# A two-block transformer kernel: expert down weights cut by output-column halves instead of rows, and the last expert finished half by half

## The chip, the cores and the metric

The kernel runs on one core of one Trainium2 chip, as one program with five instruction streams: TensorE (PE), VectorE (DVE), ScalarE (ACT), GpSimd (POOL) and SyncE (SP, which issues most transfers). The metric is the device time of one execution in microseconds. Before the change it was 996.03 us, the median of three runs (995.69 to 996.56).

## What is computed

Two blocks work on x, 256 tokens of 1024 channels, all in float32. The change lies in the last part of the second block, a mixture of 32 experts:

```python
# hn2: normed tokens; top-1 group of 4, then top-2 experts of the 8 in it
def run_block(xb, e):
    return (jax.nn.silu(xb @ w_gate[e]) * (xb @ w_up[e])) @ w_down[e]
# w_gate, w_up: (32, 1024, 512);  w_down: (32, 512, 1024)
ffn = sum over the two chosen experts of  weight * run_block(token, e)
x = x + gate2 * ffn
out = rms_norm(x, g_final)        # mean of squares over all 1024 columns
```

`gate2` is one of six pieces of 1024 columns of `silu(c) @ w_ada + b_ada`.

## The kernel before

**Stages.** The first 554 us of the profiled execution hold the first block and the attention part of the second. The rest is the expert loop (`blocks(0, NE)`, 32 experts one after the other) and a short end. A second loop, `blocks(NE, NOV)`, runs only if an expert gets more than 64 tokens; in the profiled execution it does not run.

**One expert.** Each expert has six weight pieces of 1 MB, 128 partitions of 2048 floats: four for gate and up, two for down. They lie one behind the other in `w_experts_2`, which the host lays out. SP reads them in order into 22 buffers (`er`), each used again when PE has finished with it (semaphore `eused`); late in the loop one transfer brings up to five pieces, and the last six pieces come one by one, the very last in two parts (`first0` announces its first half). On PE:

- `gate_up(j, 0)` and `gate_up(j, 1)`: 16 matmuls of 512 columns into one PSUM bank, gate in partitions 0 to 63, up in 64 to 127.
- `middle(j)`: two transposes of the product H; ACT copies the result to `HT` (`HL` for the last expert).
- `down(j)`: 8 matmuls of 512 columns. The piece `hf` holds 256 of the 512 rows of the down weights with all 1024 output columns; output columns 0 to 511 go to partitions 0 to 63 of one bank, 512 to 1023 to partitions 64 to 127.
- DVE (`down`) scales that bank by the slot weight and by gate2, ACT copies it to `Y` as a rounded high part, and DVE writes the low part `Y` (semaphore `yl`).
- `combine(j)`: four matmuls of 512 columns spread the 64 slots over the 256 tokens and add them to four banks `moe0` to `moe3` (bank `2t+q`: token half t, column half q), which hold x already. `comb_t0` and `comb` count their ends.

Every float32 matmul stands in the trace as two records with a weight load each; the two of a pair (partitions 0 to 63, and 64 to 127) run beside one another.

**The order.** It is written out by hand in `pe_program`. In the loop, `down(j - 1)` comes behind `gate_up(j, 1)` and `combine(j - 2)` before it. The end of the loop is `gate_up(31, 0)`, `middle(30)`, `combine(29)`, `gate_up(31, 1)`, first half of `down(30)`, `middle(31)`, second half of `down(30)`, `down(31)`, `combine(30)`, `combine_last(31)`. PE executes in this order, so a waiting instruction holds all behind it.

**The last expert** has no high and low parts: DVE scales its bank into `YS` in two column halves (`ys_half`, `ys`), and `combine_last` multiplies in full float32, with the partitions 0 to 63 and 64 to 127 of `YS` beside one another.

**The end.** When token half 0 is complete (`comb_t0`), ACT squares `moe0` and `moe1` with a row sum, and DVE multiplies them by g_final into `fin`, each engine one bank at a time and never the same one; then the same for token half 1 (`comb`). `mean`, `root` and `inverse` make the factor 1/rms of each token half; DVE scales the left 512 columns of `fin` and ACT the right ones; three transfers write the output, two from SP and one from ACT.

Of the kernel before, what the change touches and what calls it, by code (L numbers as in the profile page):

```python
# [8 lines left out]
F32 = DT.float32  # L9
# [4 lines left out]
ALU = mybir.AluOpType  # L14
# [6 lines left out]
NE = 32  # L21
# [81 lines left out]
class Kit:  # L103
# [331 lines left out]
    def place_psum(self):  # L435
# [104 lines left out]
        def block_uses(base, n):  # L540
            p0 = base // 4
            for q in range(4):
                use(f"gat{p0}_{q}", ((2, 3, 1, 2)[q], f"xt{q % 2}", 4 * p0 + q // 2 * 2 + 2))
            for j in range(base, base + n + 1):
                p = j // 4 + 1
                gathers = j % 4 == 3 and 4 * p < base + n
                if j < base + n:
                    use(f"gu{j}", (j % 2, "GU", j + 1))
                if j == 2:
                    use("over", (2, "count", 1))  # L550
                if j < base + n and j % 2 == 0:
                    use(f"turn{j // 2}", (3, "wsl", 2 * j + 4))
                if j > base:
                    use(f"hid{j - 1}", (2, "hf", j))
                for q in range(4 if gathers else 0):
                    use(f"gat{p}_{q}", ((j + 1) % 2, f"xt{q % 2}", 4 * p + q // 2 * 2 + 2))
                if j > base:
                    done = ("yl", 2 * self.parted(j - 1) + 2) if j < base + n else ("ys", j)
                    use(f"down{j - 1}", (3 if j < base + n else j % 2, *done))
# [5 lines left out]
def pe_program(e, K):  # L565
# [276 lines left out]
    def turn_decay():  # L842
        b = K.at["decay"][0]
        free("decay")
        for k, (row, sem, value) in enumerate((("i", "F", 2), ("w0", "E", 1))):
            e.wait_ge(S[sem], value)
            for t in range(2):
                m = e.transpose(b[:, 8 * k + 4 * t:8 * k + 4 * t + 4], K.R[row][:, 128 * t:128 * t + 128],
                                K.cst[0:4, CST["ident"]:CST["ident"] + 4])
        m.then_inc(S["dec_mm"], 1)  # L850
# [86 lines left out]
    e.matmul(K.at["shift"][0][:, 0:36], C("ones"), K.wrq[:, :], start=True, stop=True).then_inc(S["shift_mm"], 1)  # L937
# [109 lines left out]
    b = K.at["rank"][0]  # L1047
# [5 lines left out]
    def blocks(base, n):  # L1053
# [55 lines left out]
        def down(j, halves=(0, 1)):  # L1109

            if 0 in halves:
                free(f"down{j}")
                e.wait_ge(S["hf"], j + 1)
            b, HT = K.at[f"down{j}"][0], K.hidden(j)
            for hf in halves:
                i = K.piece_of[j, "d", hf]
                for c in range(2):
                    if i == K.n_static - 1 and c == 0:
                        e.wait_ge(S["first0"], 32)
                    elif c == (i == K.n_static - 1):  # L1120
                        e.wait_ge(*K.loaded(i))
                    for q in range(2):
                        m = e.matmul(b[64 * q:64 * q + 64, :], HT[:, c, hf, :],  # L1123
                                     K.weights(i)[:, 1024 * c + 512 * q:1024 * c + 512 * q + 512],
                                     start=hf == 0 and c == 0, stop=hf == 1 and c == 1)
# [12 lines left out]

        def combine_last(j):

            e.wait_ge(S["pt"], 2 * j + 2)
            e.wait_ge(S["ys_half"], 1 if j < NE else 2)
            for t, c0, c1 in ((0, 0, 256), (0, 256, 512), (1, 0, 512)):
                if c0:
                    e.wait_ge(S["ys"], j + 1)
                pt = K.PT[j % 4][:, 128 - 128 * t:256 - 128 * t]
                for q in range(2):
                    r = slice(64 * q, 64 * q + 64)
                    m = e.matmul(K.at[f"moe{2 * t + q}"][0][:, c0:c1], pt[r, :].bitcast(F32), K.YS[r, c0:c1], start=False,
                                 stop=True, skip_group_check=True)  # L1150
                if c1 == 512:
                    m.then_inc(S["comb" if t else "comb_t0"], 1)
# [6 lines left out]
        for j in range(base + 1, base + n - 1):  # L1159
# [19 lines left out]
            down(j - 1)  # L1179
# [21 lines left out]
def act_program(e, K):  # L1201
# [413 lines left out]
    def blocks(base, n):  # L1615
        def turned_p(p):
            b = K.at[f"turn{p}"][0]
            e.wait_ge(S["turnP"], p + 1)
            if p > 1:
                e.wait_ge(S["comb"], 2 * p - 2)  # L1620
            for i in range(2):
# [69 lines left out]
    with e.If(count > 0):  # L1691
        blocks(NE, NOV)
        e.wait_ge(S["comb"], NE + NOV)
# [4 lines left out]
    for t in range(2):  # L1698
        e.wait_ge(S["comb" if t else "comb_t0"], NE)
        for n in range(2):  # L1700
            if n:
                e.wait_ge(S["fin"], 2 * t + 1)
            e.activation(K.sqx[:, t, 512 * n:512 * n + 512], K.at[f"moe{2 * t + n}"][0][:, :], ACT.Square,
                         scale=1.0 / 32, accum_out=stat(8 * t + n)).then_inc(S["sq"], 1)
            if t and n == 0:
                root(11, 0, 1)
# [8 lines left out]
def dve_program(e, K):  # L1715
# [400 lines left out]
    e.wait_ge(S["dec_mm"], 1)  # L2116
# [114 lines left out]
    e.wait_ge(S["shift_mm"], 1)  # L2231
# [184 lines left out]
    def blocks(base, n, rank):  # L2416
# [31 lines left out]
        def down(j):  # L2448
            e.wait_ge(S["eused"], K.piece_of[j, "d", 1] + 1)
# [4 lines left out]
            for o, sem in ((slice(0, 256), "ys_half"), (slice(256, 512), "ys")) if whole else ((slice(0, 512), "ys"),):  # L2454
                e.scalar_tensor_tensor(out=(K.YS if whole else b)[:, o], in0=b[:, o], scalar=K.wsl[:, j % 4:j % 4 + 1],  # L2455
                                       in1=K.gate2q[:, o], op0=ALU.mult, op1=ALU.mult).then_inc(S[sem], 1)
# [50 lines left out]
    with e.If(count > 0):  # L2507
# [22 lines left out]
        blocks(NE, NOV, ok)[1]()  # L2530
        e.wait_ge(S["comb"], NE + NOV)
    finish()


    e.wait_ge(S["comb_t0"], NE)
    e.wait_ge(S["l_cst"], 32)

    def gained(t, n):
        if n == 0:
            e.wait_ge(S["sq"], 30 + 2 * t)  # L2540
# [3 lines left out]
    def mean(t):  # L2544
        k = 8 * t
        e.wait_ge(S["sq"], 31 + 2 * t)
# [8 lines left out]
    def scaled(t):  # L2555
        k = 8 * t
        e.wait_ge(S["rs"], 11 + t)
        e.wait_ge(S["fin"], 2 * t + 2)
# [197 lines left out]
def lay_out(inputs):  # L2756
# [13 lines left out]
    down = i["w_expert_down_2"][0].reshape(NE, 2, 2, 128, 1024).transpose(3, 0, 1, 2, 4)  # L2770
# [3 lines left out]
    arrays["w_experts_2"] = experts  # L2774
    arrays["norm_final_g"] = arrays["norm_final_g"].reshape(1, -1)
# [23 lines left out]
```

## Time and profile before

| quantity | value |
|---|---|
| median of 3 runs | 996.03 us (995.69 to 996.56) |
| the profiled execution's own time | 997.51 us |
| its span, first to last instruction | 995.6 us |
| mean granted TensorE clock | 0.994 |
| PE busy | 972.7 us, 98% |
| DVE / ACT busy | 57% / 42% |
| read from HBM | 326.39 MB |

The span is 1.9 us shorter than the time of the same execution; the rest lies before the first and behind the last instruction. Busy time is the union of records, and since matmuls are pipelined a busy PE need not be PE at its peak; what sets the time of a stretch is seen from the waits and from the chain. DMA and GB/s are given for 40 equal slices of 24.9 us.

### The profile page before, as it was taken

The numbers are of one execution on the slowest core, as the hardware profiler recorded it, in microseconds if no ns is written. First come the engines' busy times: TensorE is split into PE (matmuls) and PEld (weight loads), VectorE is DVE, ScalarE is ACT, GpSimd is POOL, SyncE is SP. The second block draws the span as 40 slices with busy tenths as digits, with TensorE's granted clock in tenths as the row PEclk, the third lists the DMA queues.
The fourth block names the chain that finished last, engine by engine and source line by source line (L and its number), as shares of the span: only waits on it lengthen the run. The fifth ranks groups of instructions, "written<-read, shape, count | busy, mean of one in ns | idle before, by whom it ended". The sixth has DMA issues, their size and how long they took to land.

```text
span 995.6 us, 12470 instructions
## 1 busy us (share of the span) xinstructions
PE 972.7 (98%) x4936; PEld 637.1 (64%) x4936; DVE 565.6 (57%) x883; ACT 414.6 (42%) x650; POOL 84.7 (9%) x72
## 2 busy tenths in 40 slices
PE   8999999999999999999999999999999999899986
PEld 6888888888888888889988544343434343334432
DVE  5668767898898877876986432323333222223222
ACT  6743654435644444576784423222322222122223
POOL 0122002303222202110000000000000000000000
PEclk9999999999999999999999999999999999999998
DMA  9987659995778887556558999999999999999995
GB/s 325 391 287 256 201 174 319 332 313 193 245 256 291 293 297 252 187 192 211 177 196 339 386 424 424 429 431 433 432 430 431 434 429 430 431 425 425 429 423 222
DMA packets 73599, 328.33 MB, mean 330 GB/s; under 512 B 4812, under 2 KB 4976, under 8 KB 61120
## 3 DMA queue, kind: packets, MB, share of 16 engines
q1 hardware_dynamic: 71504, 323.68, 83.1%
q0 software_dynamic: 1888, 3.54, 1.3%
q8 instruction: 41, 0.67, 0.3%
q10 hardware_dynamic: 144, 0.26, 0.1%
q14 instruction: 22, 0.18, 0.0%
HBM read 326.39 MB, written 1.07 MB: 329 GB/s over the span
## 4 chain that ended last, share of the span: by engine, by line
PE 85%; DMA 9%; DVE 3%; issue 1%; ACT 1%; SPq 0%; DVEq 0%; ACTq 0%
PE bank L1096 19%; PE bank L1123 9%; DMA er<-in_w_experts 8%; PE bank L603 7%; PE bank L606 7%; PE bank L600 7%; PE bank L786 6%; PE bank L684 5%; PE bank L1065 3%; PE bank L791 3%; PE bank L688 3%; PE bank L654 2%; PE bank L657 2%; PE bank L660 2%; PE bank L1135 2%
## 5 line engine op out<-in xcount | busy, mean ns | idle before, releaser
L1096 PE MATMUL bank<-er,XT 128*64 128x512 f32 x1024 | 235.4, 598 | 6.4 <-DMA er<-in_w_experts 6.1
L1744 DVE TENSOR_TENSOR wlo<-raw,whi 128x2048 fp32r<-128x2048 f32 x87 | 203.0, 2344 | 63.8 <-ACT whi L1209 63.6
L1209 ACT ACTIVATE whi<-raw 128x2048 fp32r<-128x2048 f32 x87 | 165.0, 1911 | 79.4 <-PE bank L606 33.7
L1096 PEld LDWEIGHTS bank<-er,XT 128*64 128x64 f32 x1024 | 70.0, 137 | 140.1 <-issue 131.2
L1123 PE MATMUL bank<-er,HT 128*64 128x512 f32 x496 | 112.3, 594 | 1.2 <-DMA er<-in_w_experts 1.2
L600 PE MATMUL bank<-whi,hh 128*128 128x512 f32 x224 | 88.4, 395 | 1.6 <-ACT whi L1216 1.6
L603 PE MATMUL bank<-wlo,hh 128*128 128x512 f32 x224 | 87.9, 393 | 0.2 <-DVE wlo L1753 0.2
L606 PE MATMUL bank<-whi,hl 128*128 128x512 f32 x224 | 88.0, 393 | 0.0
L1646 ACT ACTIVATE Y<-bank 64x512 fp32r<-64x512 f32 x62 | 36.7, 592 | 114.0 <-DVE bank L2455 113.2
L684 PE MATMUL bank<-f,whi 128*128 128x512 f32 x224 | 79.4, 398 | 0.0
L1123 PEld LDWEIGHTS bank<-er,HT 128*64 128x64 f32 x496 | 35.0, 137 | 68.6 <-issue 67.7
L1731 DVE SCALAR_TENSOR_TENSOR ada_acc<-raw,silu_c,ada_acc 128x512 f32<-128x512 f32 x96 | 75.7, 789 | 2.5
L2455 DVE SCALAR_TENSOR_TENSOR bank<-bank,wsl,gate2q 128x512 f32<-128x512 f32 x31 | 23.5, 759 | 91.3 <-PE bank L1123 91.3
L2438 DVE TENSOR_TENSOR H<-H,bank 128x256 f32<-128x256 f32 x32 | 13.5, 421 | 101.6 <-ACT H L1631 101.6
L688 PE MATMUL bank<-f,wlo 128*128 128x256 f32 x224 | 62.9, 281 | 0.0
L1631 ACT ACTIVATE H<-bank 128x256 f32<-128x256 f32 x32 | 12.3, 385 | 104.9 <-PE bank L1096 104.9
L2460 DVE TENSOR_TENSOR Y<-bank,Y 64x512 fp32r<-64x512 f32 x62 | 42.7, 689 | 21.4 <-ACT Y L1646 20.4
L786 PE MATMUL bank<-whi,zh 128*128 128x512 f32 x128 | 50.2, 392 | 0.0
L791 PE MATMUL bank<-wlo,zh 128*128 128x512 f32 x128 | 49.9, 390 | 0.0
L600 PEld LDWEIGHTS bank<-whi,hh 128*128 128x128 f32 x224 | 42.5, 190 | 10.3 <-ACT whi L1216 1.8
L684 PEld LDWEIGHTS bank<-f,whi 128*128 128x128 f32 x224 | 42.1, 188 | 10.4
L603 PEld LDWEIGHTS bank<-wlo,hh 128*128 128x128 f32 x224 | 42.4, 189 | 9.3 <-DVE wlo L1753 0.5
(387 smaller groups left out, 1581.7 us busy)
## 6 DMA issues: line engine op xcount, KB each, us to landing
er<-in_w_experts SPq DMA_DIRECT2D x27, 2048.0 KB, 37.9
er<-in_w_experts SPq DMA_DIRECT2D x49, 1024.0 KB, 9.4
er<-in_w_experts SPq DMA_DIRECT2D x12, 4096.0 KB, 33.6
raw<-in_w_in SPq DMA_DIRECT2D x41, 1024.0 KB, 6.3
er<-in_w_experts SPq DMA_DIRECT2D x8, 5120.0 KB, 28.5
raw<-in_w_ff SPq DMA_DIRECT2D x32, 1024.0 KB, 6.1
raw<-in_w_ada SPq DMA_DIRECT2D x24, 1024.0 KB, 6.2
raw<-in_w_out SPq DMA_DIRECT2D x8, 1024.0 KB, 6.8
```

What stands on the lines that cost most here:

```text
L600: e.matmul(o, a_h, r_h, start=start and c == 0, stop=False)
L603: e.matmul(o, a_h, r_l, start=False, stop=False)
L606: m = e.matmul(o, a_l, r_h, start=False, stop=stop and c == 3)
L684: e.matmul(b[q][:, :], w_h, x2[:, k, :, :].rearrange("p i n -> p (i n)"), start=k == 0, stop=False, skip_group_check=True)
L688: m = e.matmul(b[q][:, 0:256], w_l, x2[:, k, 0, :], start=False, stop=k == 7, skip_group_check=True)
L786: m = e.matmul(o, a, whi[s][:, r], start=p == 0 and f == 0 and which == 0, stop=p == 7 and f == 3 and which == 1)
L791: m = e.matmul(o, a, wlo[s][:, r], start=False, stop=False)
L1096: m = e.matmul(b[64 * w:64 * w + 64, :], K.XT[:, j % 5, k, :], K.weights(i)[:, o:o + 512], start=k == 0, stop=k == 7)
L1123: m = e.matmul(b[64 * q:64 * q + 64, :], HT[:, c, hf, :], K.weights(i)[:, 1024 * c + 512 * q:1024 * c + 512 * q + 512], start=hf == 0 and ...
L1209: e.activation(whi[K.ring(n)][:, :], raw[h.raw][:, :], ACT.Copy).then_inc(S["hi"], 1)
L1731: e.scalar_tensor_tensor(out=acc[:, :], in0=raw[h.raw][:, 512 * c:512 * c + 512], scalar=K.sc[:, 4 * k + c:4 * k + c + 1], in1=acc[:, :], ...
L1744: e.tensor_tensor(wlo[K.ring(n)][:, :], raw[h.raw][:, :], whi[K.ring(n)][:, :].bitcast(F32), ALU.subtract).then_inc(S["lo"], 1)
```

## The change

The two down pieces of an expert now hold 512 output columns each with all 512 rows, not 256 rows with all columns (`down(j, h, parts)`: piece h, four row groups g of 128). Inside a piece, columns 0 to 255 go to partitions 0 to 63 (q = 0) and 256 to 511 to partitions 64 to 127. So every matmul of `down` has 256 columns, and there are 16 of them for an expert, not 8. `combine` has eight matmuls of 256 columns, not four of 512, since a 256-column piece of Y now belongs to bank `2t + h`, columns `256q`. The host swaps the middle 256-column quarters of gate2 in `w_ada_2` and `b_ada_2` to match. Number and size of the transfers stay.

The last expert has a PSUM bank for each column half. Its two halves are computed, scaled, combined and squared one after the other. `combine_last(j, h)` has four matmuls; the third waits until the first two have ended (`comb_two`). The end works by column half: ACT squares and DVE multiplies the two token halves of columns 0 to 511 first, then of 512 to 1023; both means come at the end. Two single-use semaphores are merged into `small_mm`, which changes no order.

```diff
-        def down(j, halves=(0, 1)):
...
-            for hf in halves:
-                i = K.piece_of[j, "d", hf]
-                for c in range(2):
...
-                    for q in range(2):
-                        m = e.matmul(b[64 * q:64 * q + 64, :], HT[:, c, hf, :],
-                                     K.weights(i)[:, 1024 * c + 512 * q:1024 * c + 512 * q + 512],
+        def down(j, h, parts=range(4)):
+            use, whole = K.at[f"down{j}"], j == base + n - 1
...
+            b, HT, i = use[h if whole else 0], K.hidden(j), K.piece_of[j, "d", h]
+            for g in parts:
+                if i == K.n_static - 1 and g < 2:
+                    e.wait_ge(S["first0"], 32)
+                else:
+                    e.wait_ge(*K.loaded(i))
+                for q in range(2):
+                    m = e.matmul(b[64 * q:64 * q + 64, 256 * h:256 * h + 256], HT[:, g % 2, g // 2, :],
+                                 K.weights(i)[:, 512 * g + 256 * q:512 * g + 256 * q + 256],
...
         def combine(j):
...
-                    m = e.matmul(K.at[f"moe{2 * t + q}"][0][:, :], K.PT[j % 4][:, 128 - 128 * t:256 - 128 * t], K.Y[q][:, :],
-                                 start=False, stop=False, skip_group_check=True)
+                    for h in range(2):
+                        m = e.matmul(K.at[f"moe{2 * t + h}"][0][:, 256 * q:256 * q + 256],
+                                     K.PT[j % 4][:, 128 - 128 * t:256 - 128 * t], K.Y[q][:, 256 * h:256 * h + 256],
...
+        def combine_last(j, h):
+            if h:
+                e.wait_ge(S["ys"], j + 1)
+            else:
+                e.wait_ge(S["pt"], 2 * j + 2)
+                e.wait_ge(S["ys_half"], 1 if j < NE else 2)
+            for n, (t, q) in enumerate(((0, 0), (1, 1), (0, 1), (1, 0))):
+                if n == 2:
+                    e.wait_ge(S["comb_two"], 6 * (j // NE) + 3 * h + 2)
+                r = slice(64 * q, 64 * q + 64)
+                m = e.matmul(K.at[f"moe{2 * t + h}"][0][:, 256 * q:256 * q + 256],
+                             K.PT[j % 4][r, 128 - 128 * t:256 - 128 * t].bitcast(F32), K.YS[r, 256 * h:256 * h + 256],
+                             start=False, stop=True, skip_group_check=True)
+                m.then_inc(S["comb_two" if n < 3 else "comb" if h else "comb_t0"], 1)
...
-        down(j - 1, (0,))
+        down(j - 1, 0)
         middle(j)
-        down(j - 1, (1,))
-        down(j, (0, 1))
+        down(j - 1, 1)
+        down(j, 0)
         combine(j - 1)
-        combine_last(j)
+        down(j, 1, (0, 1))
+        combine_last(j, 0)
+        down(j, 1, (2, 3))
+        combine_last(j, 1)
...
# ACT, the end
-    for t in range(2):
-        e.wait_ge(S["comb" if t else "comb_t0"], NE)
-        for n in range(2):
-            if n:
-                e.wait_ge(S["fin"], 2 * t + 1)
+    for n in range(2):
+        e.wait_ge(S["comb_two"], 3 * n + 3)
+        e.wait_ge(S["comb" if n else "comb_t0"], NE)
+        for t in range(2):
+            if t:
+                e.wait_ge(S["fin"], 2 * n + 1)
...
# DVE, the end
-    gained(0, 1)
+    gained(1, 0)
     gained(0, 0)
-    mean(0)
+    e.wait_ge(S["comb_two"], 6)
     e.wait_ge(S["comb"], NE)
     gained(1, 1)
-    gained(1, 0)
+    gained(0, 1)
+    mean(0)
+    mean(1)
     inverse(0)
-    mean(1)
     scaled(0)
```

On PE, at the end of the loop from `down(31)` on, stood before (L1123 is `down`, L1135 `combine`, L1149 `combine_last`; HL is the last expert's hidden tile, Y and YS the scaled results, PT the slot-to-token matrix; x3 means three more of the kind):

```order
L1123 MATMUL bank<-er_187,HL 64x512 [waits e_10,hf,GU]
L1123 MATMUL bank<-er_187,HL 64x512 x3
L1123 MATMUL bank<-er_187,HL 64x512 [waits first0]
L1123 MATMUL bank<-er_187,HL 64x512
L1123 MATMUL bank<-er_187,HL 64x512 [waits e_whi0]
L1123 MATMUL bank<-er_187,HL 64x512
L1135 MATMUL bank<-Y_175,PT_181 128x512 [waits yl,pt]
L1149 MATMUL bank<-YS,PT_182 128x256 [waits ys_half,pt]
L1149 MATMUL bank<-YS,PT_182 128x256
L1149 MATMUL bank<-YS,PT_182 128x256 [waits ys]
L1149 MATMUL bank<-YS,PT_182 128x256
L1149 MATMUL bank<-YS,PT_182 128x512 x2
```

At the same place, from the first matmul of `combine(30)` on, now stands (L1140 is `combine`, L1126 `down`, L1156 `combine_last`; before these rows lie the eight matmuls of `down(31, 0)`, and seven more L1140 follow its first row):

```order
L1140 MATMUL bank<-Y_175,PT_181 128x256 [waits yl,pt]
L1126 MATMUL bank<-er_187,HL 64x256 [waits first0,hf,GU]
L1126 MATMUL bank<-er_187,HL 64x256 [waits first0]
L1156 MATMUL bank<-YS,PT_182 128x256 [waits ys_half,pt]
L1156 MATMUL bank<-YS,PT_182 128x256 [waits comb_two]
L1126 MATMUL bank<-er_187,HL 64x256 [waits e_whi0,hf]
L1126 MATMUL bank<-er_187,HL 64x256 [waits e_whi0]
L1156 MATMUL bank<-YS,PT_182 128x256 [waits ys]
L1156 MATMUL bank<-YS,PT_182 128x256 [waits comb_two]
```

`combine(30)` has moved from behind all of `down(31)` to behind its first half, and the second half of `down(31)` now stands behind that wait for `yl`, cut in two by the first half of `combine_last`.

On DVE, at the end, stood before (L2455 scales the last expert's halves, L2541 multiplies by g_final, L2547 is `mean`, L2553 `inverse`, L2559 `scaled`):

```order
L2455 SCALAR_TENSOR_TENSOR YS<-bank,wsl,gate2q 128x256 [waits yl,wsl,eused]
L2455 SCALAR_TENSOR_TENSOR YS<-bank,wsl,gate2q 128x256
L2541 TENSOR_TENSOR fin<-bank,gfb 128x512 [waits l_cst,comb_t0]
L2541 TENSOR_TENSOR fin<-bank,gfb 128x512 [waits sq]
L2547 SCALAR_TENSOR_TENSOR st<-st 128x1 [waits sq]
L2541 TENSOR_TENSOR fin<-bank,gfb 128x512 [waits comb]
L2541 TENSOR_TENSOR fin<-bank,gfb 128x512 [waits sq]
```

and now stands (L2476 scales, L2564 multiplies, L2570 is `mean`):

```order
L2476 SCALAR_TENSOR_TENSOR YS<-bank,wsl,gate2q 128x256 [waits eused,yl,wsl]
L2476 SCALAR_TENSOR_TENSOR YS<-bank,wsl,gate2q 128x256 [waits eused]
L2564 TENSOR_TENSOR fin<-bank,gfb 128x512 [waits l_cst,comb_t0,comb_two]
L2564 TENSOR_TENSOR fin<-bank,gfb 128x512 [waits sq]
L2564 TENSOR_TENSOR fin<-bank,gfb 128x512 [waits comb,comb_two]
L2564 TENSOR_TENSOR fin<-bank,gfb 128x512 [waits sq]
L2570 SCALAR_TENSOR_TENSOR st<-st 128x1 [waits sq] x2
```

The second scaling has a wait of its own, for the second column half of `down(31)`, and all multiplications by g_final stand behind it.

## Rows read from the trace of the kernel before

**Rows 1.** The page: slices of 24.9 us, DMA share in tenths and rate.
```profile
DMA  9987659995778887556558999999999999999995
GB/s 325 391 287 256 201 174 319 332 313 193 245 256 291 293 297 252 187 192 211 177 196 339 386 424 424 429 431 433 432 430 431 434 429 430 431 425 425 429 423 222
```

**Rows 2.** PE's waits, 556 to 985 us: total us, times, longest.
```profile
PE bank L1096 <- DMA er<-in_w_experts: 6.1, 4, 3.7
PE bank L1123 <- DMA er<-in_w_experts: 1.2, 1, 1.2
```

**Rows 3.** Stretches: from:to, length, busy us by engine, granted clock, DMA share, GB/s.
```profile
855.30:859.60 4.30, 0.59 (x6) 0.02 (x2) 1.38 (x2) 0.88 (x2) 0.00 (x0) 1.00 1.01 434
859.60:864.00 4.40, 4.40 (x16) 2.12 (x17) 0.00 (x0) 0.00 (x0) 0.00 (x0) 0.61 1.00 432
963.07:967.97 4.90, 3.65 (x16) 1.26 (x17) 0.76 (x1) 0.42 (x1) 0.00 (x0) 1.00 0.99 415
967.97:982.40 14.43, 14.43 (x66) 5.32 (x68) 3.02 (x5) 2.99 (x7) 0.00 (x0) 1.00 0.93 384
```

**Rows 4.** The chain that ended last: start us, us, what.
```profile
516.64 2.75 PE bank L924 x32
563.10 3.58 PE bank L1096 x16
587.29 3.43 PE bank L1123 x16
865.73 1.21 PE bank L1065 x8
985.17 1.09 PE bank L1149 x8
```

**Rows 5.** Groups by form, L924 and L1149: count, busy us, mean ns.
```profile
L924 PE MATMUL bank<-PTt,vat 128*64 128x256 f32 x16 | 2.5, 385 | 0.0
L924 PE MATMUL bank<-PTt,vat 128*64 128x128 f32 x16 | 1.6, 272 | 0.0
L1149 PE MATMUL bank<-YS,PT 64*128 64x256 f32 x8 | 1.1, 402 | 0.0
```

**Rows 6.** Timeline of PE, a gather and a combine: start us, us, what.
```profile
561.89 0.39 PE L1065 MATMUL bank<-PP,th 128*128 128x256 f32 x1
...
563.03 3.65 PE L1096 MATMUL bank<-er,XT 128*64 128x512 f32 x16
...
971.76 1.17 PE L1135 MATMUL bank<-Y,PT 128*128 128x512 f32 x4
...
972.86 3.65 PE L1096 MATMUL bank<-er,XT 128*64 128x512 f32 x16
```

**Rows 7.** Timeline of all engines, 980 us to the end.
```profile
980.39 3.65 PE L1123 MATMUL bank<-er,HL 128*64 128x512 f32 x16
981.93 1.41 DVE L2460 TENSOR_TENSOR Y<-bank,Y 64x512 fp32r<-64x512 f32 x2 [0.66 <-ACT Y L1646]
982.76 0.40 PEld L1123 LDWEIGHTS bank<-er,HL 128*64 128x64 f32 x4 [0.46 <-DMA er<-in_w_experts]
983.97 1.20 PE L1135 MATMUL bank<-Y,PT 128*128 128x512 f32 x4
984.08 0.88 DVE L2455 SCALAR_TENSOR_TENSOR YS<-bank,wsl,gate2q 128x256 f32<-128x256 f32 x2 [0.74 <-PE bank L1123]
985.10 1.99 PE L1149 MATMUL bank<-YS,PT 64*128 64x256 f32 x12
986.28 1.42 DVE L2541 TENSOR_TENSOR fin<-bank,gfb 128x512 f32<-128x512 f32 x2 [1.32 <-PE bank L1149]
989.54 1.32 ACT L1710 ACTIVATE fin<-fin,st 128x512 f32<-128x512 f32 x2
989.92 0.49 DVE L2559 TENSOR_SCALAR fin<-fin,st 128x512 f32<-128x512 f32 x1
990.49 1.80 SPq L2723 DMA_DIRECT2D out<-fin  x1
```

More of the change, by code:

```diff
@@ L557, in block_uses @@
                 if j > base:
-                    done = ("yl", 2 * self.parted(j - 1) + 2) if j < base + n else ("ys", j)
-                    use(f"down{j - 1}", (3 if j < base + n else j % 2, *done))
+                    if j < base + n:
+                        use(f"down{j - 1}", (3, "yl", 2 * self.parted(j - 1) + 2))
+                    else:
+                        use(f"down{j - 1}", (0, "ys_half", 1 if base == 0 else 2), (1, "ys", j))
         block_uses(0, NE)
@@ L936, in pe_program @@
     e.wait_ge(S["router"], ROUTER["sum"])
-    e.matmul(K.at["shift"][0][:, 0:36], C("ones"), K.wrq[:, :], start=True, stop=True).then_inc(S["shift_mm"], 1)
+    e.matmul(K.at["shift"][0][:, 0:36], C("ones"), K.wrq[:, :], start=True, stop=True).then_inc(S["small_mm"], 1)
     def turn_h(t):
@@ L1134, in combine @@
                 for q in range(2):
-                    m = e.matmul(K.at[f"moe{2 * t + q}"][0][:, :], K.PT[j % 4][:, 128 - 128 * t:256 - 128 * t], K.Y[q][:, :],
-                                 start=False, stop=False, skip_group_check=True)
+                    for h in range(2):
+                        m = e.matmul(K.at[f"moe{2 * t + h}"][0][:, 256 * q:256 * q + 256],
+                                     K.PT[j % 4][:, 128 - 128 * t:256 - 128 * t], K.Y[q][:, 256 * h:256 * h + 256],
+                                     start=False, stop=False, skip_group_check=True)
                 m.then_inc(S["comb" if t else "comb_t0"], 1)
[L1139 to L1152, printed above, removed]
+        def combine_last(j, h):
+            if h:
+                e.wait_ge(S["ys"], j + 1)
+            else:
+                e.wait_ge(S["pt"], 2 * j + 2)
[8 more added lines that the diff above has]
+                m.then_inc(S["comb_two" if n < 3 else "comb" if h else "comb_t0"], 1)
         gather(base // 4, 0)
@@ L1184, in blocks @@
         gate_up(j, 1)
-        down(j - 1, (0,))
+        down(j - 1, 0)
         middle(j)
-        down(j - 1, (1,))
-        down(j, (0, 1))
+        down(j - 1, 1)
+        down(j, 0)
         combine(j - 1)
-        combine_last(j)
+        down(j, 1, (0, 1))
+        combine_last(j, 0)
+        down(j, 1, (2, 3))
+        combine_last(j, 1)
     e.wait_ge(S["tl"], 2)
@@ L2453, in down @@
             b, whole = K.at[f"down{j}"][0], j == base + n - 1
-            for o, sem in ((slice(0, 256), "ys_half"), (slice(256, 512), "ys")) if whole else ((slice(0, 512), "ys"),):
-                e.scalar_tensor_tensor(out=(K.YS if whole else b)[:, o], in0=b[:, o], scalar=K.wsl[:, j % 4:j % 4 + 1],
-                                       in1=K.gate2q[:, o], op0=ALU.mult, op1=ALU.mult).then_inc(S[sem], 1)
+            if not whole:
+                e.wait_ge(S["eused"], K.piece_of[j, "d", 1] + 1)
+                e.scalar_tensor_tensor(out=b[:, :], in0=b[:, :], scalar=K.wsl[:, j % 4:j % 4 + 1], in1=K.gate2q[:, :],
+                                       op0=ALU.mult, op1=ALU.mult).then_inc(S["ys"], 1)
+            if whole and base:
+                e.wait_ge(S["comb_two"], 6)
+            for h in range(2 if whole else 0):
+                o = slice(256 * h, 256 * h + 256)
+                e.wait_ge(S["eused"], K.piece_of[j, "d", h] + 1)
+                e.scalar_tensor_tensor(out=K.YS[:, o], in0=K.at[f"down{j}"][h][:, o], scalar=K.wsl[:, j % 4:j % 4 + 1],
+                                       in1=K.gate2q[:, o], op0=ALU.mult, op1=ALU.mult).then_inc(S["ys" if h else "ys_half"], 1)
             for q in range(0 if whole else 2):
@@ L2530, in dve_program @@
         blocks(NE, NOV, ok)[1]()
+        e.wait_ge(S["comb_two"], 12)
         e.wait_ge(S["comb"], NE + NOV)
     finish()
+    e.wait_ge(S["comb_two"], 3)
     e.wait_ge(S["comb_t0"], NE)
@@ L2774, in lay_out @@
     arrays["w_experts_2"] = experts
+    for name in ("w_ada_2", "b_ada_2"):
+        gate = arrays[name][..., 5120:6144]
+        gate = gate.reshape(*gate.shape[:-1], 2, 2, 256).swapaxes(-3, -2).reshape(gate.shape)
+        arrays[name] = np.ascontiguousarray(np.concatenate([arrays[name][..., 0:5120], gate], axis=-1))
     arrays["norm_final_g"] = arrays["norm_final_g"].reshape(1, -1)
```

38 lines of the change are left out of this document (18 added, 20 removed).

## The prediction

> **What bounds the kernel now.** I read the slices of the page first, then PE's waits, the stretches, the chain, and last the timeline of the end. The slices show two regimes: before slice 22 the transfer rate varies, from slice 24 (about 600 us) on it stays at 424 to 434 GB/s with a DMA share of nine tenths or more [rows 1]. From there to the end of the expert weights the transfers are at their rate. PE is almost as full: from 556 to 985 us it waits for weights five times, 7.3 us in all (6.1 + 1.2) [rows 2]. So the expert loop is held by the transfers, with PE 7.3 us short of holding it itself. The reader is to see that the last such wait ends at 967.97 us (1.25 us of the 4.90 us from 963.07 are free of PE work) and that PE then works without a break: 14.43 us busy in 14.43 us [rows 3]. What is behind 967.97 us is PE's, and at its very end a chain over PE, DVE and ACT. The last weights arrive when the load at 982.76 us is released, and its matmuls start 0.2 us later, so in the last expert transfers and PE are level [rows 7].
>
> **The change in the loop.** The matmuls of down get twice as many and half as wide. Before, the 16 records of an expert (512 columns each) take 3.43 us, and 0.15 us more when matmuls of another shape stand before them (3.58) [rows 4]; that is 8192 record columns, 0.42 ns each. No row shows 32 records of 256 columns with 64 weight columns, but L924 has this shape: 16 records of 256 and 16 of 128 columns, 6144 record columns, in 2.75 us [rows 4, 5]. At 0.42 ns they cost 2.57 us; with the entry of 0.15 us that leaves 0.03 us over 32 records. Lower bound of the extra: nothing. Upper bound: L924's whole rate, 2.75 / 6144 x 8192 = 3.67 us, so +0.24 us. I take +0.03, because L924 contains one entry, which down has already.
>
> Combine goes from four matmuls of 512 columns to eight of 256. The gather L1065 has just this shape and number. Start to next line's start it takes 563.03 - 561.89 = 1.14 us, the combine before takes 972.86 - 971.76 = 1.10 us [rows 6]: +0.04 us. The bound below is zero, since the columns are the same; the bound above is twice the matmuls at the old cost each, +1.1 us, which the gather rules out; with a wait before it the gather takes 1.21 us [rows 4], so +0.11 at most.
>
> Together +0.07 us an expert, 29 experts before 967.97 us: 2.0 us of PE work, 10 us at the upper ends (0.24 + 0.11). The 7.3 us in which PE waits for weights hide the 2.0 us. The cover is gone from 0.25 us an expert on; at the upper ends 2.9 us would come through. There is also work to get back: after the wait of 3.7 us the granted clock is 0.61 for 4.4 us, which is near the lower level, 1.2 GHz, and PE had been idle before it fell [rows 3]; a shorter wait there may keep it at 2.4 GHz. Number, size and order of transfers stay. So up to 967.97 us: zero.
>
> The Trainium skill (TensorE: Matmul & The Clock Gate, section "The mechanism") says that a weight load overlaps running matmuls only when its row group differs. All of down's matmuls use all rows. By that rule none of its loads would be hidden, and twice the loads would cost twice the load time. The trace disagrees: 16 records with a load each take exactly the time of their columns, and L924 at half the width nearly so [rows 4, 5]. What the rule would give is the fourth case below.
>
> **The change in the end.** I go through PE's order, before and after.
> 1. down(31) starts at 980.39 us [rows 7]; after it is +0.07 (combine(29) and down(30)): 980.46.
> 2. Its first half takes 1.72 us: PE is through at 982.2.
> 3. Next in PE's queue is combine(30), which waits for `yl`. DVE finishes it at 981.93 + 1.41 = 983.34 us [rows 7], after down(30), ACT's copy and two subtractions, which the change leaves as they are; +0.06 makes 983.40. Before, the 3.65 us of down(31) covered this. Now PE stands 1.2 us, and the second half of down(31), which needs nothing from DVE, stands behind it. PE goes on at 983.45 (a handover is 0.04 to 0.05 us, as from PE's end 984.04 to DVE's start 984.08 [rows 7]).
> 4. combine(30), eight matmuls behind a wait: 1.21 us [rows 4]: 984.66.
> 5. Two of four row groups of the second half: entry 0.15 + 0.86 = 1.01: 985.67.
> 6. combine_last(31, 0). `ys_half` is ready (DVE 983.4 + 0.44). Eight records of this kind take 1.09 us, 0.54 for four, and one lasts 0.40 [rows 4, 5]. The third matmul waits for the ends of the first two: 0.27 + 0.40 + 0.05 = 0.72, then 0.54: 986.93.
> 7. The other two row groups: 0.15 + 0.86, and 0.22 until the last result stands (3.65 against 3.43): 988.16. The data came at 982.8, it does not matter here.
> 8. DVE scales half 1: 0.44 us, with two handovers 0.53: 988.69.
> 9. combine_last(31, 1): 0.72 + 0.27 + 0.40 = 1.39: 990.1 us. Before, the last combine ended at 985.10 + 1.99 = 987.09 [rows 7]. That is **+3.0 us**, of it 1.2 from the wait in 3, 0.9 from the two waits of PE for itself (0.45 each), the rest from DVE's scaling, which now lies alone between two pieces of PE work, and from entries.
>
> Then the column order should pay. ACT squares token half 0 of columns 0 to 511 at 987.2, but the square of token half 1 waits for DVE's first product, and DVE's queue has the scaling of step 8 before it: product 988.7 to 989.4 (0.71 [rows 7]), second square to 990.1. So the first half is just off the path at 990.1. Behind the last combine: square, square, 0.70 each, with handovers to 991.6; means, root and reciprocal to 992.25 (0.65); scaling of the left columns 0.49, reciprocal, scaling 0.49: 993.35. Before, the last scaling ended at 989.92 + 0.49 = 990.41, 3.32 us behind the last combine; now 3.25. The last SP transfer, which waits for it, moves from 990.49 to 993.4. ACT's right half moves from 990.86 (989.54 + 1.32) to 993.55. Gain of the new order 0.1 to 0.2 us.
>
> **Sum:** 0 + 3.0 - 0.15 = **+2.85 us**, take 2.8. The profiled execution goes from 997.51 to 1000.3 (span 998.4); it stands 1.48 us above the median, so the median goes from 996.03 to **998.8 us**. Bounds of the end: if PE's self-waits cost nothing and entries neither, +1.5; if a half combine takes 0.3 more each time, +3.5.
>
> **Rivals.**
> *No change.* The wait for `yl` or the self-waits are cheaper than I read. Without the 1.2 and the 0.9 the sum is +0.7 us, 996.7. Against it: DVE's 983.34 is a measured end and PE cannot pass it.
> *The half order wins (not slower).* Its place is the last landing L. From L to the last combine the old order needs 987.09 - 982.76 = 4.3 us; the new one, if PE stands ready at step 7's matmuls, needs 1.2 + 0.53 + 1.4 = 3.1 and then 0.1 less: 1.3 us gained, 994.7 us. PE reaches these matmuls at 986.9, so this holds in full only if weights land after 987, and it breaks even at L = 990.1 - 4.3 - 0.1 = 985.7, 3 us later than the trace has it. For it: transfers are the bound of the whole loop. Against it: their rate and bytes stay, and the trace has them in at 982.8.
> *PE becomes the bound of the loop.* If narrow matmuls cost the upper ends, 2.9 us come through on top: 1001.7. If loads do not hide (the page's rule, worked out as a mechanism of this kernel: eight more pairs of loads an expert, each as long as the load group at 982.76 for four, 0.40, thus 0.2 a pair), 1.6 us an expert, 51 us, less 7.3: 1043 us. L924 speaks against both.
>
> **How the numbers follow.** About 2 us, 0.2%, is what a measurement of this kernel can tell from no change. Forecast 78% (with its own spread of 0.8 us, a sixth of it below +2 us); no change 10%; half order wins 6%; PE the bound 6%, of it one for unhidden loads. Slower by over 0.2%: 0.65 + 0.06 = 0.71. Faster: 0.04, from the third case with a late landing and from errors in all steps. Same: 0.25. The range reaches from the no-change case less some scatter, 996.3, to just under the upper ends, 1001.4.
>
> **What would show it.** In the changed profile: down's 32 records an expert in 3.4 to 3.5 us; waits for weights in the loop 4 to 6 us in all, not 7.3; the last group of them still ending near 968 us; a PE wait at `combine` (L1140) for DVE `Y` of about 1.2 us near 983; last combine near 990.1; span near 998.4. I am wrong if PE starts gate_up(31, 0) later than 968.5, if there is no PE idle time between 982 and 983.4, if the last combine ends before 989, or if the rate of the last slices differs.

## The result, and the profile after

The changed kernel takes 1000.66 us in the median of six runs (999.2 to 1003.5), the kernel before 996.15 us (six runs): ratio 1.0046, 95% interval 1.0035 to 1.0056. It is slower by 4.5 us. Two more series, r1 and r3 below, gave 1.0038 (1.0022 to 1.0055) and 1.0030 (1.0020 to 1.0041), 3 to 4 us. A ratio of 1.0010 is 1 us. The ratios are not the quotients of the medians; for a kernel with few runs the two can differ by 0.0017, and where they tell different things both are given. Times and ratios here are of runs in the fast state; one run of before (1167 us) and one of loop_only (2176 us) in series r3 were slow. The forecast was 998.8 us, +2.8; the time of 1000.66 us lies inside the range, near its upper end.

The profiled execution took 999.30 us, with a span of 997.5 us. The page, slices of 24.9 us as in [rows 1]:

```profile
DMA  9987559985688886655658999999999999999994
GB/s 330 391 305 257 184 169 352 327 297 207 211 287 300 298 277 231 221 195 172 211 204 324 394 424 423 427 439 428 426 434 426 439 424 431 433 423 426 426 423 172
```

From slice 23 on the transfers run at 423 to 439 GB/s, as before. PE's waits from 556 to 988 us, against [rows 2] (L1098 is gate_up, L1140 combine, L1126 down):

```profile
PE bank L1098 <- DMA er<-in_w_experts: 5.8, 3, 3.3
PE bank L1140 <- DVE Y L2481: 1.3, 1, 1.3
PE bank L1126 <- DMA er<-in_w_experts: 1.0, 1, 1.0
```

There are still 6.8 us of waits for weights (before: 7.3), and one new wait, for Y. The groups by form, against [rows 4, 5]:

```profile
L1126 PE MATMUL bank<-er,HT 128*64 128x256 f32 x992 | 112.9, 380 | 1.0 <-DMA er<-in_w_experts 1.0
L1140 PE MATMUL bank<-Y,PT 128*128 128x256 f32 x248 | 37.0, 291 | 1.3 <-DVE Y L2481 1.3
```

The same view of the kernel before has 112.3 and 36.4 us for these two groups, at half the count (496 and 124). Twice the matmuls at half the width cost 0.6 us and 0.6 us over the whole loop, so 0.02 us each an expert.

The end of the loop and the end, against [rows 7] (timeline: start us, us, engine, line, operation; L1156 is combine_last, L2476 the scaling of a column half, L2564 the product with g_final):

```profile
967.42 3.65 PE L1098 MATMUL bank<-er,XT 128*64 128x512 f32 x16 [1.24 <-DMA er<-in_w_experts]
...
979.80 1.95 PE L1126 MATMUL bank<-er,HL 128*64 128x256 f32 x16
...
981.50 1.41 DVE L2481 TENSOR_TENSOR Y<-bank,Y 64x512 fp32r<-64x512 f32 x2 [0.66 <-ACT Y L1659]
...
983.06 1.19 PE L1140 MATMUL bank<-Y,PT 128*128 128x256 f32 x8 [1.31 <-DVE Y L2481]
...
984.18 1.08 PE L1126 MATMUL bank<-er,HL 128*64 128x256 f32 x8
...
985.19 1.50 PE L1156 MATMUL bank<-YS,PT 64*128 64x256 f32 x8
...
986.62 1.08 PE L1126 MATMUL bank<-er,HL 128*64 128x256 f32 x8
...
987.75 0.48 DVE L2476 SCALAR_TENSOR_TENSOR YS<-bank,wsl,gate2q 128x256 f32<-128x256 f32 x1 [4.26 <-PE bank L1126]
988.15 1.28 DVE L2564 TENSOR_TENSOR fin<-bank,gfb 128x512 f32<-128x512 f32 x2
988.29 1.50 PE L1156 MATMUL bank<-YS,PT 64*128 64x256 f32 x8 [0.59 <-DVE YS L2476]
...
993.03 0.46 SPq L2747 DMA_DIRECT2D out<-fin  x1
```

The reader is to see three things. The last wait for weights ends at 967.42 us, not later than before (967.97). PE stands 1.31 us before combine(30), while the second half of down(31) is behind it in the queue. And PE then hands to DVE and takes back (987.70 to 988.29). From 967.42 to the issue of the last SP transfer, 993.03, are 25.61 us; before it is 990.49 - 967.97 = 22.52 us [rows 3, 7]. So this chain is **3.1 us** longer. In this pair of executions the spans differ by 1.9 us only: the changed kernel's chain began 0.55 us sooner, and what comes behind the last issue was 0.65 us shorter. The kernel before has a single trace, and it is 1.4 us above its median of 996.15 us; so the chains can be compared with it, but what differs before and behind the chain can't be read from this pair.

PE's wait for itself is in the waits of 979 to 990 us:

```profile
PEld bank L1140 <- issue: 1.7, 1, 1.7
PE bank L1140 <- DVE Y L2481: 1.3, 1, 1.3
PEld bank L1156 <- DVE YS L2476: 1.0, 1, 1.0
PEld bank L1156 <- PE bank L1156: 1.0, 2, 0.5
```

The last row is the third matmul of each combine_last, held until the first two have ended: twice 0.5 us in which no weights are loaded.

### The profile page after: what moved, and what is told of

It is laid out like the page before. It is cut to its first block and busy times, and to the rows that moved or that the text cites. A ratio compares the mean times of both kernels' runs of the same rounds, so it can differ in the third digit from the quotient of the medians.

```text
span 997.5 us, 13786 instructions
## 1 busy us (share of the span) xinstructions
PE 974.4 (98%) x5576; PEld 684.0 (69%) x5576; DVE 565.8 (57%) x883; ACT 415.1 (42%) x650; POOL 84.8 (9%) x72
## 5 line engine op out<-in xcount | busy, mean ns | idle before, releaser
L1098 PE MATMUL bank<-er,XT 128*64 128x512 f32 x1024 | 236.1, 600 | 6.1 <-DMA er<-in_w_experts 5.8
L1098 PEld LDWEIGHTS bank<-er,XT 128*64 128x64 f32 x1024 | 70.3, 137 | 122.3 <-issue 107.3
L1126 PE MATMUL bank<-er,HT 128*64 128x256 f32 x992 | 112.9, 380 | 1.0 <-DMA er<-in_w_experts 1.0
L1126 PEld LDWEIGHTS bank<-er,HT 128*64 128x64 f32 x992 | 70.9, 137 | 46.9 <-issue 15.1
```

The lines of the kernel that those rows point to most:

```text
L1098: m = e.matmul(b[64 * w:64 * w + 64, :], K.XT[:, j % 5, k, :], K.weights(i)[:, o:o + 512], start=k == 0, stop=k == 7)
L1126: m = e.matmul(b[64 * q:64 * q + 64, 256 * h:256 * h + 256], HT[:, g % 2, g // 2, :], K.weights(i)[:, 512 * g + 256 * q:512 * g + 256 * q ...
```

## The experiments

Theory A: PE's order at the end makes the change slower, the loop costs nothing since it waits for weights. Theory B: the narrow matmuls in the loop cost time. As a third case from the prediction: the new order pays if the weights come late.

The labels r1, r2 and r3 name three series; all kernels of a series ran on one chip beside the kernel before, each series on another chip. The table holds the traced pieces: from gate_up(31, 0), where the last wait for weights ends, to down(31) (I), to the end of combine_last (II), to the issue of the last SP transfer (III), their sum, and from there to the end of the span (IV). Where a kernel was traced more than once, the values of I to III agreed within 0.04 us.

| kernel | I | II | III | sum | IV | ratio to before (95%) |
|---|---|---|---|---|---|---|
| before | 12.42 | 6.70 | 3.40 | 22.5 | 5.1 | |
| loop_only | 12.42 | 6.74 | 3.40 | 22.6 | 4.6, 4.9 | 1.0006 (0.9996 to 1.0015), 1.0018 (1.0006 to 1.0030) |
| old_order | 12.40 | 7.49 | 3.30 | 23.2 | 5.7, 5.2 | 1.0026 (1.0014 to 1.0037), 1.0024 (1.0015 to 1.0033) |
| interleaved | 12.37 | 6.75 | 4.11 | 23.2 | 5.8 | 1.0015 (1.0003 to 1.0028) |
| covered | 12.40 | 8.17 | 3.24 | 23.8 | 5.9 | 1.0019 (1.0002 to 1.0035) |
| comb_late | 12.37 | 8.99 | 3.24 | 24.6 | 5.6, 4.3 | 1.0049 (1.0033 to 1.0066), 1.0042 (1.0029 to 1.0055) |
| changed | 12.39 | 9.98 | 3.24 | 25.6 | 4.5, 4.4, 5.4 | 1.0046, 1.0038, 1.0030 (as above) |

**The changed kernel again**, unedited, twice.

> The changed kernel, unedited, for more executions and a second trace. The first trace explains +2.5 us of the end (last expert's first matmul 979.80 to span 997.5: 17.7 us; before 980.39 to 995.6: 15.2), while the median of six is +4.5 us. Theory A (the end alone, plus now and then a stretch of lower granted clock): this trace again has 17.5 to 18 us from that matmul to the end, and what is above lies in a stretch of clock 0.5 to 0.6 that the other trace lacks, or in a later last wait for weights. Theory B (the loop is slower): the last expert starts over 1 us later than 980.4 with the clock at 1.0 throughout. Median 999.5 to 1001.5.

> The changed kernel once more, to pool its time with the two series before. Theory A (its trace: +3.1 us from the last wait for weights to the issue of the last output transfer, 25.61 against 22.52 us): ratio to before 1.003 to 1.004, and those 25.6 us again. Theory B (a further cost that the traces do not show): 1.0045 or more again.

Medians 1000.25 and 999.03 us. The chain is 25.61 and 25.63 us, so what the trace shows of the end is the same each time; neither shows a stretch of low clock that would explain more. Theory A stands for the chain. The +3.0 us of r3 is the chain's +3.1; of the +3.8 us of r1 and the +4.5 us of the result, 0.7 and 1.4 us are not covered by it.

**loop_only**: the kernel before with narrow matmuls and nothing else.

```diff
-                    for q in range(2):
-                        m = e.matmul(b[64 * q:64 * q + 64, :], HT[:, c, hf, :],
-                                     K.weights(i)[:, 1024 * c + 512 * q:1024 * c + 512 * q + 512],
+                    for s_ in range(2):
+                        for q in range(2):
+                            o = 1024 * c + 512 * q + 256 * s_
+                            m = e.matmul(b[64 * q:64 * q + 64, 256 * s_:256 * s_ + 256], HT[:, c, hf, :],
+                                         K.weights(i)[:, o:o + 256],
...
# combine: likewise, two matmuls of 256 columns for each of 512
```

> The kernel before with only the narrow matmuls of the change: down 16 matmuls of 256 columns, combine eight of 256, same row pieces, same order, same end. Theory A: the loop's extra PE work (0.035 us an expert in the first trace) lies under the waits for weights, so within 0.4 us of before: 996.2 to 996.6. Theory B (narrow matmuls cost time that the one trace did not show, by longer loop or lower clock): +1.5 to +2.5 us, 997.7 to 998.7.

> Narrow matmuls alone, once more. Theory A: ratio 1.0000 to 1.0005, 22.6 us from the last wait for weights to the last output issue. Theory B (narrow matmuls carry the part of the cost that is missing in the traces): 1.001 or more.

The chain is 22.6 us, like before. The times are 996.75 us (before 996.7) in r1 and 997.12 us (before 995.75) in r3: +0.6 us by the ratio (-0.4 to 1.5) in the one series, +1.8 us (0.6 to 3.0) in the other. One of the eleven runs of r3, 1001.51 us, had a granted clock of 0.947, where the others have 0.994 to 0.998; it raises the second ratio. By the bounds set ahead of it, r3 came out as Theory B said (1.001 or more) and r1 as Theory A did. So the traces say that the narrow matmuls cost the chain nothing, and the times leave room for about 1 us outside it. A cost of that size is neither shown nor excluded.

**old_order**: the changed kernel with PE's old order; column pieces, combining and squaring by column half stay.

```diff
         down(j, 0)
+        down(j, 1)
         combine(j - 1)
-        down(j, 1, (0, 1))
         combine_last(j, 0)
-        down(j, 1, (2, 3))
         combine_last(j, 1)
```

> The changed kernel with PE's old order at the end: down(31) whole, combine(30), then both halves of combine_last; column pieces, narrow matmuls, combining and squaring by column half stay. Theory A (+3.0 us of the end come from PE's wait for Y, and DVE's second scaling alone between pieces of PE work): no wait for Y, DVE scales both halves under combine(30); last combine at 987.7 to 988.0, 2.0 us less than the changed kernel, +0.7 to +1.0 us against before. Rival (narrow matmuls and column order cost it, not PE's order): stays within 0.7 us of the changed kernel.

> Column pieces with PE's old order, once more. Theory A (its trace: 23.2 us from the last wait to the last output issue, +0.7 over before): +0.5 to +1.2 us over before in time. Rival (its first series, +2.6 us, holds; the column pieces cost 1 to 2 us outside the traced chain): +2 us or more again.

```profile
982.84 1.01 DVE L2475 SCALAR_TENSOR_TENSOR YS<-bank,wsl,gate2q 128x256 f32<-128x256 f32 x2
983.26 1.22 PE L1140 MATMUL bank<-Y,PT 128*128 128x256 f32 x8
984.41 2.73 PE L1156 MATMUL bank<-YS,PT 64*128 64x256 f32 x16
986.04 2.71 DVE L2563 TENSOR_TENSOR fin<-bank,gfb 128x512 f32<-128x512 f32 x4 [2.19 <-PE bank L1156]
...
990.44 0.39 SPq L2746 DMA_DIRECT2D out<-fin  x1
```

In the chain Theory A is right: the wait for Y is gone, DVE scales both halves under combine(30), and of the 3.1 us 2.4 are back. In time it is 2.0 us (1000.25 to 998.29) and 0.75 us (999.03 to 998.28) faster than the changed kernel by the medians, 1.2 and 0.6 us by the ratios. Against before it is 2.6 and 2.4 us slower by the ratios, where the chain says 0.7. So the rival of r3, that the column pieces cost 1 to 2 us outside the traced chain, came out as it was written; what that cost is stays open.

**comb_late**: combine(30) behind two more row groups.

```diff
         down(j, 0)
-        combine(j - 1)
         down(j, 1, (0, 1))
+        combine(j - 1)
         combine_last(j, 0)
```

> The changed kernel with combine(30) moved behind the first two row groups of the second half of down(31). Theory A (PE's 1.3 us wait for Y holds these matmuls back): they fill the wait, 0.9 to 1.0 us less than the changed kernel. Rival (what sets the end is not PE but DVE's and ACT's queue behind the scaling): under 0.3 us less.

> combine(30) behind the first two row groups of the second half, once more, since its first series scattered over 4.5 us. Theory A (its trace: 1.0 us less than the changed kernel up to the last output issue, 24.6 us): 0.7 to 1.3 us faster than r3_after. Rival: no faster than r3_after again, then the gap is given back in the output transfers.

The wait falls from 1.31 to 0.47 us, and combine_last ends 0.99 us sooner, as expected:

```profile
979.99 2.81 PE L1126 MATMUL bank<-er,HL 128*64 128x256 f32 x24
...
983.27 1.18 PE L1140 MATMUL bank<-Y,PT 128*128 128x256 f32 x8 [0.47 <-DVE Y L2481]
```

The time does not follow: 999.84 and 1000.04 us, against 1000.25 and 999.03 us of the changed kernel, so no faster. I had expected 0.7 to 1.3 us. For the first trace a part of it is seen behind the last issue, below; for the second it is not, and no run explains it.

**interleaved**: old order, and the pairs of the two halves of combine_last in turn, so that PE never waits for itself.

```diff
+        down(j, 1)
         combine(j - 1)
...
+        combine_last(j, 0, (0,))
+        combine_last(j, 1, (0,))
+        combine_last(j, 0, (1,), 2)      # comb_two >= 2
+        combine_last(j, 1, (1,), 4)      # comb_two >= 4
...
# combine_last takes the pairs it issues; ACT and DVE wait for 5 and 6 of comb_two, not 3 and 6
```

> Old order on PE (down(31) whole, combine(30)), and the two halves of combine_last interleaved, pair 1 of half 0, pair 1 of half 1, pair 2 of half 0, pair 2 of half 1, so that PE never waits for its own matmuls. Theory A: against r1_old_order (7.49 us from down(31)'s first matmul to the end of combine_last) two self-waits of 0.4 us go: 6.7 to 6.9 us, like the kernel before (6.70); 0.7 us faster than r1_old_order, within 0.5 us of before. Rival (the column pieces and the end by column half cost more than PE's order): the trace is as said, but the time stays at r1_old_order's +1.5 to +2.5 us over before.

combine_last ends 6.75 us behind down(31)'s first matmul, 0.74 us sooner than in old_order; that is what two self-waits are worth on PE. Nothing of it arrives: piece III grows from 3.30 to 4.11 us. The ends of PE's and DVE's work show why:

```profile
983.92 2.00 PE L1158 MATMUL bank<-YS,PT 64*128 64x256 f32 x16
985.62 2.71 DVE L2567 TENSOR_TENSOR fin<-bank,gfb 128x512 f32<-128x512 f32 x4 [2.26 <-PE bank L1158]
...
990.03 0.39 SPq L2750 DMA_DIRECT2D out<-fin  x1
```

The four products take 2.71 us without a gap from 985.62 us on. The first column half is ready only 0.3 us before the second. From down(31)'s first matmul (979.17 us) to the first product it is 6.45 us, in old_order 6.39 us (979.65 to 986.04), so the first half comes no sooner; and from there to the last SP issue it is 4.41 us here and 4.40 us there. So in both kernels the path runs from the first half on over DVE and ACT, not over PE, and in old_order the self-wait in the second half was hidden already. In time it is 1.6 us slower than before (997.84 against 996.24 us), which is the rival's case: the trace as said, the time not back.

**covered**: the new order without its self-wait in the first half, the second pair of combine_last(31, 0) behind the last row groups of down, and combine(30) as in comb_late.

```diff
         down(j, 0)
-        combine(j - 1)
         down(j, 1, (0, 1))
-        combine_last(j, 0)
+        combine(j - 1)
+        combine_last(j, 0, (0,))
         down(j, 1, (2, 3))
+        combine_last(j, 0, (1,))
         combine_last(j, 1)
...
# combine_last takes the pairs it issues
```

> The changed kernel's idea without two of its waits: down(31) first half and two row groups, combine(30), first pair of combine_last(31, 0), last two row groups, second pair of combine_last(31, 0), combine_last(31, 1). Theory A: from down(31)'s first matmul to the end of combine_last 8.99 us (r1_comb_late) less one self-wait, 8.5 to 8.7; the remaining +1.9 over before are the wait for Y (0.5), DVE's lone scaling (1.0 with the self-wait that follows) and shape entries. Rival: PE's self-wait had been hidden, then 9.0.

8.17 us, 0.3 to 0.5 less than expected: besides the self-wait, the pair now runs while DVE scales the second half. In the chain this is the best of the new order's three versions, 0.6 us behind old_order and 1.3 us behind before. By time it can't be told from old_order: 1.0019 (1.0002 to 1.0035) against 1.0026 and 1.0024. Its expectation had said 8.5 to 8.7 us, its rival 9.0; it was neither.

**Late weights.** SP issues 2 MB of other transfers (1.5 MB to unused places, and g_final) before the second half of the last weight transfer, once in the kernel before and once in the changed one.

```diff
             e.dma_start(K.weights(i)[:, 0:1024], src[:, 0:1024]).then_inc(S["first0"], 16)
+            e.wait_ge(S["gat"], NE)
+            e.dma_start(K.pad0[:, :], A["w_experts_2"][:, 1, 0, :]).then_inc(S["s_out"], 16)
+            e.dma_start(K.pad1[:, :], A["w_experts_2"][:, 2, 0, 0:1024]).then_inc(S["s_out"], 16)
+            e.dma_start(K.gfb[:, :], A["g_final_2"].broadcast_to([128, 1024])).then_inc(S["l_cst"], 16)
             e.dma_start(K.weights(i)[:, 1024:2048], src[:, 1024:2048]).then_inc(sem, 16)
...
# the transfer of g_final behind the loop goes; two unused places are declared
```

> The kernel before with the second half of its last weight transfer made late: SP issues 1.5 MB of transfers to unused places and the 0.5 MB of g_final ahead of it, 2 MB at 0.43 MB/us, so that it lands 4.9 us later, near 988. Theory A: the old end needs 4.3 us from the last landing to the end of combine_last, which ends near 992: +4.5 to +5 us over before.

> The changed kernel with the same late last transfer. Theory A: PE's waits of the new order now lie before the landing; from it to the end of combine_last 3.1 us, near 991, +1 to +1.5 us over the changed kernel and 0.8 to 1.5 us faster than r2_before_late: the new order pays only for late weights. Rival (the new order is worse wherever the weights land): slower than r2_before_late by 0.5 us or more.

Medians 1003.22 us (ratio 1.0054, 1.0033 to 1.0074) and 1000.4 us (1.0039, 1.0027 to 1.0052): now the changed order is the faster one, by 2.8 us in the medians and 1.5 us in the ratios, whose intervals overlap. The timelines, first of before with late weights, then of the changed kernel with late weights:

```profile
980.49 2.80 PE L1125 MATMUL bank<-er,HL 128*64 128x512 f32 x12
...
987.82 1.98 PE L1125 MATMUL bank<-er,HL 128*64 128x512 f32 x4 [4.53 <-DMA er<-in_w_experts]
989.72 2.08 PE L1137 MATMUL bank<-Y,PT 128*128 128x512 f32 x4
...
997.64 0.39 SPq L2727 DMA_DIRECT2D out<-fin  x1
```

```profile
986.09 1.08 PE L1128 MATMUL bank<-er,HL 128*64 128x256 f32 x8 [0.60 <-DMA er<-in_w_experts]
...
992.49 0.40 SPq L2751 DMA_DIRECT2D out<-fin  x1
```

The old order stands 4.53 us in one piece before its last matmuls. The new one has work until the landing and waits 0.60 us. From the end of the last wait at gate_up(31, 0) to the last SP issue it is 29.6 us (968.07 to 997.64) against 26.3 us (966.22 to 992.49): the new order wins 3.3 us. I had worked out 1.3 for the full case; the rest is the clock, which fell to its lower level in the old order's long wait. From its landing to the end of combine_last the old order takes 6.42 us (987.82 to 994.24), where the kernel before takes 4.3, so 2.1 of the 3.3 us are the clock. Stretches of before with late weights, columns as in [rows 3]:

```profile
983.30:987.80 4.50, 0.00 (x0) 0.00 (x0) 0.13 (x1) 0.81 (x2) 0.00 (x0) 0.80 0.36 147
987.80:991.20 3.40, 3.38 (x8) 1.46 (x8) 0.88 (x2) 0.00 (x0) 0.00 (x0) 0.50 0.00 0
```

At 0.50, 1.2 GHz, the combine takes 2.08 us and not 1.20. The landing itself, counted from the end of the last wait at gate_up(31, 0), is at 19.75 us in the one and 19.87 us in the other, so the comparison is a fair one.

## Why the prediction came out as it did

**The loop: right.** 0.07 us an expert was forecast, all hidden. Measured are 0.04 (two groups, 0.02 each), hidden: the last wait for weights ends at 966.2 to 967.8 us in all traces of the changed end. The granted clock after the long wait fell in the first trace and not in the two others (below), without any effect on the last wait: from the loop's first gate_up matmul to the end of that wait it is 412.5, 412.4 and 412.5 us. The fourth case, loads that are not hidden, is refuted by the 112.9 us. The waits for weights are 6.8 us in the first trace and 8.8 and 8.9 us in the two others, all outside my 4 to 6. The loop began at 554.6 to 555.3 us in these traces and at 557.0 us in the one of before, so PE came to the weights earlier and waited longer, and in the first trace the low clock filled a part of the waits; I had taken the start for given.

**The wait for Y: right.** 1.2 us forecast, 1.31 measured. DVE finishes at 981.50 + 1.41 = 982.91 us, PE goes on at 983.06, and moving combine(30) behind 0.86 us of matmuls (comb_late) takes 0.84 of the wait away. The case of no change, which needed this wait or the self-waits to be cheap, is refuted by the two.

**The self-waits and DVE's lone scaling: right in kind, a little small.** I had the end of PE's combine_last 9.6 us behind down(31)'s start; it is 9.98. The missing 0.4 us are three pieces. combine(30) starts 3.26 us behind down(31), not 2.99: Y is finished 0.17 us later, and PE starts 0.15 us behind DVE's end, where I had put 0.05 from a handover in the other direction. DVE's turn takes 0.59 us instead of 0.53, and the last combine_last 1.50, not 1.39. What lies between is 0.07 us shorter than forecast. The two self-waits, forecast at 0.9 us together, are 0.74 us by interleaved. So the 3.3 us by which PE's end moves (9.98 against 6.70) are 1.3 for Y, 0.7 for the self-waits, 0.6 for DVE's turn, and an estimated 0.6, the difference, for entries after another shape.

**The end behind it: right.** Forecast 0.1 to 0.2 us gained, measured 0.16 (3.24 against 3.40). covered and interleaved show why the column order brings no more: the first half's products are off the path in the one, and the path moves to DVE and ACT in the other.

**The sum.** +2.85 forecast, +3.1 in the traced chain, +3.0 to +4.5 in time. Of the 1.7 us by which the time of the result passes the forecast (4.5 against 2.8), 0.3 are the chain's and 1.4 lie outside it: I set everything outside the chain to zero. By the ratios, the kernels with narrow matmuls measure 0.5 to 2.8 us more than their chains, comb_late most; the exceptions are the changed kernel in r3 (0.1 less) and with late weights (0.1 more). But the kernel before with late weights, whose matmuls are wide, has a chain 7.05 us longer than before and a ratio of only +5.4 us (+7.0 in the medians), so differences of 1 to 2 us between a chain and a time are not all the change's. For old_order and comb_late the excess is beyond the interval in both series, 1.7 to 2.8 us. Its cause is not settled. One piece of it is seen in the traces, in the last section, but I have not shown that it is the whole.

**The rival "half order wins": right as a mechanism.** It decides with the landing: with the last piece early, at 982.8 us, the order loses 3.1 us; late enough that PE would wait, it wins 3.3 us, of which 2.1 are the clock that the old order lost in its wait and that the forecast of 1.3 did not have. The turning point that I forecast, a landing at 985.7 us, was not tried.

**The signs of being wrong.** None of the four appeared: gate_up(31, 0) starts at 967.42 us, PE is idle up to 983.06 us, the last combine ends at 989.79 us, and the rates up to the last full slice are those of before.

## What to carry to other kernels

Before a wait is put ahead of independent work in an in-order queue, look when it will be released: combine(30) was moved 1.7 us forward in the queue and started only 0.3 us sooner, since Y was finished 3.1 us behind down(31)'s start, in both kernels within 0.2 us; most of the rest, 1.3 us, became a wait in front of matmuls that needed nothing from DVE. Splitting the last piece into halves paid where the engine would otherwise wait for that piece; where it was busy until the data came, each split added handovers (0.4 us for a wait on the own result, 0.6 us for a turn over DVE). Halving a matmul's columns from 512 to 256 at the same total cost 0.04 us an expert in the traces. And a chain read from a trace is not the whole time: in old_order 2.4 us of the chain came back and 0.6 to 2.0 us of the time.

## What the runs showed of the hardware

**An instruction fetch beside the output transfers.** The last SP issue to the end of the span takes 3.9 to 5.9 us for the same 1.05 MB of output. In the packet records the program's own fetches (queue q8, "instruction"; one packet of 16 KB each, 0.9 to 2.1 us long) differ in place. In six traces one starts 0.4 to 2.7 us behind the last SP issue; these take 5.2 to 5.9 us (old_order twice, interleaved, covered, comb_late's first, the changed kernel's third). In the other eight none starts there, and they take 3.9 to 5.1 us: in four of them one starts 3.3 to 3.5 us behind the issue, when the output is nearly through (4.3 to 4.5 us), in three one starts up to 0.15 us ahead of it (4.6 to 5.1 us), and in one the last starts 1.0 us ahead (3.9 us). The transfers of the third trace of the changed kernel and of the first, from 993.3 us in 40 equal slices of 0.14 us:

```profile
GB/s 0 15 336 424 351 351 307 483 322 366 395 336 366 380 395 336 366 366 395 366 322 293 88 15 29 29 29 15 29 29 29 15 29 0 0 0 0 0 0 0
```

```profile
GB/s 380 395 351 293 249 293 351 410 410 351 410 410 351 410 395 366 380 366 351 351 74 117 0 0 0 0 0 0 0 0 0 0 0 0 0 0 0 0 0 0
```

In the first, a fetch began at 994.3 us; the bulk ends at 996.5 us, and for 1.4 us more a trickle of 15 to 29 GB/s is left, about one sixteenth of the 430 GB/s of the loop (27), as if one of the 16 engines were behind the others. In the second all end together. This fits fourteen traces but was not tried by itself: the fetch is an argued cause, not a shown one. It would explain why comb_late's 1.0 us does not arrive in its first trace (5.6 us); its second has 4.3.

**The clock after a wait of 3.3 us.** Twelve traces have the same wait of 3.3 us at gate_up near 858 us. Behind it the granted clock fell to 0.50 in nine and stayed at 1.00 in three (covered and the changed kernel's second and third). Stretches of the changed kernel's first and of its second trace:

```profile
858.30:862.00 3.70, 3.68 (x9) 0.84 (x9) 0.00 (x0) 0.00 (x0) 0.00 (x0) 0.50 1.01 434
```

```profile
859.00:864.00 5.00, 4.71 (x34) 3.47 (x32) 1.37 (x4) 0.40 (x2) 0.00 (x0) 1.00 0.97 419
```

From PE's restart to the first matmul of the next `middle` it is 2.92 us in the three traces at full clock, 4.5 to 4.6 us in eight of the nine, and 5.49 us in the changed kernel's first, where the clock was low for longer. So the same wait cost PE nothing, 1.6 or 2.6 us; the waits for weights behind it hid that here.
